# Recurrent mixer: running sums spread over the partitions by bf16 products of three exact pieces, dt from split weights, the selection table written on the chip

## The reference, cut to what matters

```python
proj = h @ w_in
z, xbc, dt, hq, hf, hi, hg = split_cols(proj, [...])        # dt: 8 columns, one for each head
xbc = silu(causal_depthwise_conv_2(xbc, conv_w, conv_b))
...
dt = softplus(dt.astype(F32) + dt_bias.astype(F32))
a_head = -exp(a_log.astype(F32))
a = (dtc * a_head...)                                        # 8 heads x 256 tokens
a_cs = cumsum(a, axis=-1)
seg = exp(where(causal, a_cs[..., :, None] - a_cs[..., None, :], -inf))
y_diag = einsum('bcgls,bcgrls,bcsgrp->bclgrp', cb, seg, xh)
```

## Time and profile before

| | |
|---|---|
| median of 3 runs | 971.42 us (971.24 to 971.78) |
| profiled execution | span 969.5 us; its whole time is not among the numbers, the runs lie 1.9 us above the span |
| PE busy | 951.9 us, 98% |
| DVE, ACT, POOL busy | 697.7, 521.5, 85.5 us |
| recurrent mixer | about 641 to 775 us of the span |

### The profile page before, as it was taken

The page is one execution under the profiler, slowest core; times in us unless marked ns, Lnnn a source line. Parts: engine busy times, 40 slices in busy tenths (PEclk is TensorE's granted clock), DMA queues, the critical chain, the costliest instruction groups (busy, mean ns, idle before and its releaser), DMA issues.

```text
span 969.5 us, 13640 instructions
## 1 busy us (share of the span) xinstructions
PE 951.9 (98%) x5566; PEld 833.2 (86%) x5566; DVE 697.7 (72%) x922; ACT 521.5 (54%) x707; POOL 85.5 (9%) x110
## 2 busy tenths in 40 slices
PE   9999999999999999999999999999999999999997
PEld 8998888888888798789988888888988798888885
DVE  5889866666658977877676666667989777666663
ACT  5888564444446556865444434368555454443432
POOL 2541100000011100000000000000132110000000
PEclk9999999999999999999999999999999999999999
DMA  9922566556645454145655565557322446756531
GB/s 302 318 94 98 191 222 217 174 182 205 198 153 196 129 165 171 47 131 174 217 174 188 186 192 178 168 172 216 114 88 75 143 143 213 224 184 193 181 122 44
DMA packets 106190, 164.40 MB, mean 170 GB/s; under 512 B 2816, under 2 KB 82784, under 8 KB 106000
## 3 DMA queue, kind: packets, MB, share of 16 engines
q1 hardware_dynamic: 104688, 158.25, 50.8%
q0 software_dynamic: 1440, 5.28, 1.5%
HBM read 162.47 MB, written 1.05 MB: 169 GB/s over the span
## 4 chain that ended last, share of the span: by engine, by line
PE 80%; DVE 12%; ACT 4%; issue 2%; POOL 1%; DMA 0%; SPq 0%; DVEq 0%; ACTq 0%
PE ps L379 78%; DVE wl L1770 3%; PE ps L387 2%; ACT xhl L1195 1%; ACT junk L1177 1%; POOL st L2559 1%; DVE st L2192 1%; DVE xf L1791 1%; DVE xhl L1787 1%; DVE rows L2395 1%; DVE h L1844 1%; DVE hs L1802 1%; DMA prm<-in_prm 0%; ACT SC L1515 0%; DVE hs L2406 0%
## 5 line engine op out<-in xcount | busy, mean ns | idle before, releaser
L1770 DVE TENSOR_TENSOR wl<-raw,wh 128x2048 fp32r<-128x2048 f32 (+2 forms) x146 | 329.8, 2262 | 142.0 <-ACT wh L1189 141.8
L1189 ACT ACTIVATE wh<-raw 128x2048 fp32r<-128x2048 f32 (+2 forms) x150 | 281.8, 1884 | 151.7 <-PE ps L379 144.1
L379 PE MATMUL ps<-xhl,wh 128*128 128x512 f32 (+1 forms) x1248 | 254.7, 350 | 0.3 <-ACT wh L1254 0.3
L379 PEld LDWEIGHTS ps<-xhl,wh 128*128 128x128 f32 x1248 | 199.3, 190 | 27.8 <-issue 1.1
L379 PE MATMUL ps<-wh,xhl 128*128 128x512 f32 (+3 forms) x1000 | 195.5, 339 | 1.6 <-issue 0.9
L379 PEld LDWEIGHTS ps<-wh,xhl 128*128 128x128 f32 x1000 | 155.3, 190 | 20.4 <-issue 1.3
L379 PEld LDWEIGHTS ps<-xhl,wl 128*128 128x128 f32 x1008 | 135.7, 191 | 7.5
L379 PE MATMUL ps<-xhl,wl 128*128 128x256 f32 x1008 | 140.6, 282 | 0.0
L379 PE MATMUL ps<-wl,xhl 128*128 128x512 f32 (+3 forms) x500 | 105.4, 336 | 1.0 <-DVE wl L1770 0.9
L379 PE MATMUL ps<-wh,fh 128*128 128x512 f32 x304 | 91.3, 392 | 1.0 <-DVE fl L2034 0.7
L379 PE MATMUL ps<-wh,fl 128*128 128x512 f32 x304 | 90.4, 390 | 0.0
(11 more groups left out here) (274 smaller groups left out, 840.0 us busy)
## 6 DMA issues: line engine op xcount, KB each, us to landing
raw<-in_ffn_gate SPq DMA_DIRECT2D x22, 1024.0 KB, 5.5
raw<-in_ffn_up SPq DMA_DIRECT2D x22, 1024.0 KB, 5.5
raw<-in_ffn_down SPq DMA_DIRECT2D x22, 1024.0 KB, 4.9
raw<-in_w_up SPq DMA_DIRECT2D x16, 1024.0 KB, 5.6
raw<-in_w_down SPq DMA_DIRECT2D x16, 1024.0 KB, 5.0
raw<-in_s_w_in SPq DMA_DIRECT2D x14, 1024.0 KB, 5.4
raw<-in_w_in SPq DMA_DIRECT2D x9, 1024.0 KB, 9.5
raw<-in_a_w_in SPq DMA_DIRECT2D x6, 1024.0 KB, 5.3
```

The costliest lines, as they stand in the source:

```text
L379: return e.matmul(o, a, b, start=start, stop=stop, skip_group_check=True)
L1189: e.activation(high_of(i), raw_of(i), ACT.Copy).then_inc(*up("act_high", i))
L1770: e.tensor_tensor(low_of(i), raw_of(i), high_of(i).bitcast(F32), ALU.subtract).then_inc(*up("dve_lo", i))
```

## The change

Three parts. (1) dt: ACT rounds `wdt` (64 columns) to `wdt_h`, the DVE takes the rest to `wdt_l`, and the PE makes three passes of eight fp32r products with 128 columns of weights each (8 wanted, the rest zeros or other rows that nobody reads). (2) seg: POOL cuts the 8 x 256 running sums into three bf16 pieces in four dependent steps; the first piece lies in rows 0 to 7 of `T3`, the DVE copies the others to rows 32 to 39 and 64 to 71; `sel` has ones in these three rows for a head, so one bf16 product adds the pieces in float32. (3) The float32 table leaves `cst` (1600 columns that POOL's queue loads become 576), `prm` grows from 201 to 209 columns, and POOL writes `sel` (128 x 1024 bf16) and zeros to `T3` and the tails of `wdt_h` and `wdt_l` at the start of the first MLP.

```diff
 # PE, recurrent
-                e.wait_ge(*at("dma_wdt"))
-                e.wait_ge(*at("dve_h", 5, 1, 1))
-                for k in range(8):
-                    d = mm(ps[0][0:8, 0:256], wdt[:, k, :], xf[:, k, :], k == 0, k == 7)
+                for n, (w, x) in enumerate(((wdt_h, xh), (wdt_h, xl), (wdt_l, xh))):
+                    if n != 1:
+                        e.wait_ge(*(at("dve_dt_low") if n else at("act_dt_high")))
+                    for k in range(8):
+
+                        d = mm(ps[0][:, 0:256], w[:, 8 * k:8 * k + 128], x[:, k, :], n == 0 and k == 0, n == 2 and k == 7)
...
                 def seg(i):
-                    o, sel = ps[SEG_BANK[i]], cst[:, C_SEL + 128 * i:C_SEL + 128 * i + 128]
+
+                    o = ps[SEG_BANK[i]]
+                    if i == 0:
+                        e.wait_ge(*at("pool_sel"))
+                        e.wait_ge(*at("pool_seg_high"))
+                        e.wait_ge(*at("dve_seg_rows", 1))
...
-                    mm(o[:, 0:256], sel, T2, True, False)
+                    mm(o[:, 0:256], sel[:, i, :], T3[:, :], True, False)
                     mm(o[:, 0:128], idb[:, :], mtb[:, :], False, True)
-                    mm(o[:, 256:384], sel, T2[:, 128:256], True, False)
+                    mm(o[:, 256:384], sel[:, i, :], T3[:, 128:256], True, False)
 # ACT, after norm_high(5, 1)
+                e.wait_ge(*at("dma_wdt"))
+                e.wait_ge(*at("pool_zero_pieces"))
+                e.activation(wdt_h[:, 0:64], wdt, ACT.Copy).then_inc(*up("act_dt_high"))
 # DVE, before the wait for pe_dt
+                e.wait_ge(*at("act_dt_high"))
+                e.tensor_tensor(wdt_l[:, 0:64], wdt, wdt_h[:, 0:64].bitcast(F32), ALU.subtract).then_inc(*up("dve_dt_low"))
 # DVE, after conv(0)
+                e.wait_ge(*at("pool_seg_rest"))
+                for i, x in enumerate((middle, rest)):
+                    e.tensor_copy(T3[32 + 32 * i:40 + 32 * i, :], x[R, :]).then_inc(*up("dve_seg_rows", i))
 # POOL, after the load of pT (first MLP)
+            e.tensor_copy(sel[:, :, :], P("sel", 0, 8).unsqueeze(2).to_broadcast([128, 8, 128])).then_inc(*up("pool_sel"))
+            for x in (wdt_h, wdt_l):
+                e.memset(x[:, 64:184].bitcast(F32), 0.0)
+            e.memset(T3[:, :], 0.0).then_inc(*up("pool_zero_pieces"))
 # POOL, after the load of hm (recurrent mixer)
+            R = slice(0, 8)
+            e.wait_ge(*at("dve_dt_sum"))
+            e.tensor_copy(T3[R, :], T2[R, :]).then_inc(*up("pool_seg_high"))
+            e.wait_ge(*at("pool_seg_high"))
+            e.tensor_tensor(rest[R, :], T2[R, :], T3[R, :], ALU.subtract).then_inc(*up("pool_seg_left"))
+            e.wait_ge(*at("pool_seg_left"))
+            e.tensor_copy(middle[R, :], rest[R, :]).then_inc(*up("pool_seg_middle"))
+            e.wait_ge(*at("pool_seg_middle"))
+            e.tensor_tensor(rest[R, :], rest[R, :], middle[R, :], ALU.subtract).then_inc(*up("pool_seg_rest"))
```

More of the change, by code:

```diff
@@ L24 @@
 TAPS = 31
-C_ID, C_MA, C_MT, C_ONE, C_SEL, C_ROPE = 0, 128, 256, 384, 512, 1536
+C_ID, C_MA, C_MT, C_ONE, C_ROPE = 0, 128, 256, 384, 512
 C_N = C_ROPE + 2 * 96
@@ L33 @@
           ("qn", 3), ("kvn", 2), ("subln", 1), ("s_norm", 4), ("g_norm", 1), ("lb0", 4), ("lb1", 4),
-          ("bf", 1), ("dtb", 1), ("alog", 1), ("fsel", 4), ("eps", 1), ("mhalf", 4)]
+          ("bf", 1), ("dtb", 1), ("alog", 1), ("fsel", 4), ("eps", 1), ("mhalf", 4), ("sel", 8)]
 P_AT = {}
@@ L48 @@
                       "act_exp act_map_turned act_latent_out act_back"),
-    "act_recurrent": ("act_bound act_hq act_forget act_keys act_log_forget act_rate act_z act_hi act_decay act_between "
+    "act_recurrent": ("act_bound act_dt_high act_hq act_forget act_keys act_log_forget act_rate act_z act_hi act_decay act_between "
                       "act_xbc act_hg act_xb act_xs act_cb act_seg act_gated_square act_silu"),
@@ L56 @@
                       "dve_map dve_map_diff dve_diff_out dve_latent_x dve_latent_low dve_k_rope dve_mix2_low"),
-    "dve_recurrent": ("dve_bound dve_forget_gate dve_keys dve_floor dve_ones dve_decay_sum dve_dt_rate dve_dt_ones "
+    "dve_recurrent": ("dve_bound dve_dt_low dve_seg_rows dve_forget_gate dve_keys dve_floor dve_ones dve_decay_sum dve_dt_rate dve_dt_ones "
                       "dve_dt_sum dve_dt_cumulated dve_score dve_weighed dve_conv_tap dve_conv dve_dt_turned dve_decayed "
@@ L148, in program @@
         mtb = sb("mtb", [128, 128], BF16)
+        sel = sb("sel", [128, 8, 128], BF16)
+        T3 = sb("T3", [128, 256], BF16)
+        middle = sb("middle", [128, 256], BF16)
+        rest = sb("rest", [128, 256])
+        wdt_h, wdt_l = (sb(n, [128, 184], F32R) for n in ("wdt_h", "wdt_l"))
         st = sb("st", [128, 96])
@@ L248, in program @@
         At = fl_f[:, 1280:1360].rearrange("p (a b) -> p a b", a=2)
-        wdt = fl_f[:, 1360:1424].rearrange("p (a b) -> p a b", a=8)
+        wdt = fl_f[:, 1360:1424]
         ones = QK[:, 0, 0:256]
@@ L2702, in constants @@
     c[:, C_ONE:C_ONE + 128] = f(1.0 / 256)
-    for n in range(8):
-        c[n, C_SEL + 128 * n:C_SEL + 128 * n + 128] = 1
     pos = np.arange(256, dtype=f)
@@ L2757 @@
         prm[i, P_AT["fsel"] + i] = prm[32 + i, P_AT["fsel"] + i] = 1
+    for n in range(8):
+        prm[n:96:32, P_AT["sel"] + n] = 1
     prm[:, P_AT["eps"]] = EPS
```

## The result

The changed kernel takes 973.21 us (median of 9 runs; without one disturbed run at 5372 us, which is left out from here on, 973.19), the kernel before 971.55 (9 runs, 971.24 to 971.78): a ratio of 1.0024, 95% interval 1.0015 to 1.0032. The eight runs that are left have two levels, which the kernel before hasn't: five at 973.02 to 973.21 and three at 974.70 to 974.95. The profiled execution is one of the lower level (973.16, span 971.4); so I took the two apart: **some 1.5 us that every run pays** (the middle of the lower five is 973.06; 1.6 by the traces), and **another 1.7 to 1.8 us that some pay**.

What follows compares the result with a forecast made beforehand. The PE sets the end up to 709.8 us, then the DVE; ahead of cb the PE has 1.0 us of room. Mixer +0.66 and first MLP +0.05 make +0.7 on 971.4: 972.1 us, range 970.3 to 973.7.

Steps and rivals of the forecast that it cites:

- sel and the fills in the first MLP: POOL's cast starts after the DVE's L1770 ends, fills only write: cost 0 to 0.2 us, taken as 0.05.
- if the DVE's row around 121 us grows by over 0.3: One of three signs that the prediction is wrong, at the start of the first MLP.
- the PE's wait ahead of cb: In the recurrent mixer, PE waits for ACT some 2 us where there was no wait before.
- POOL's steps: Two subtractions and two casts from 667.4 us in the recurrent mixer, 2.45 us together.
- price d: DVE time lost beside POOL's steps from 667.4 us: 1.5 us, 0.61 of their time; bounds 0.5 to 2.9.
- the standstill of the rival: DVE stands still for the whole of each POOL step it meets: 2.45 us lost, time 973.1; chance 0.15.
- The copies: Two 8 x 256 copies on the DVE after conv(0): 0.45 us, all falling on the last SiLU.
- The DVE took back 0.28: DVE's wait for ACT at 673.39 us follows the PE, now early, so 0.28 us of the loss returns.
- The scans of G: DVE scans in the recurrent mixer, at 675.8 us before, were to come 1.2 us later.
- The last SiLU: ACT's step after the convolution, needed by cb: 1.67 us later, at hand at 702.51.
- cb: late by 0.66: PE's cb waits for the last SiLU, 702.51 against 701.85 us; the first weigh moves by the same 0.66 us.
- seg(2) to seg(7): Some 3 us less PE time in the ladder, where the DVE has no room: taken as 0.

Runs made afterwards that it cites:

- experiment 1: Kernel before plus only POOL's unused 128 x 1024 cast behind the load of pT: 973.07 us; with a fill of that size instead: 972.22 us.
- late table: Changed kernel with POOL's cast of sel and fills behind one more wait, well into the first MLP: seven runs at 971.35 to 971.84 us, four at 972.87 to 972.99.

## Why the prediction was wrong, and where it was right

**The failed step** is "*sel and the fills in the first MLP* ... it starts when that has ended ... Cost 0 to 0.2, I take 0.05". It measured 1.6 us (experiment 1), which is the whole loss that every run pays. I took the order from the rows of before: L1770 starts at 118.84, the cast can't start before the load of pT is issued (its record says 119.38), so the DVE would be first. That order was turned over by a step that I hadn't looked at, the pair on hs at 118.04. Its second half is held until about 119.2 (experiment 1, by cast and fill alike), so L1770 comes to its turn only at 119.63, behind the cast, and stands still for the cast's rest. Half of the loss is the pair, half is L1770, and the forecast had the wrong engine wait. That POOL's step holds the pair before its own recorded start was in no row of before; that no wait guards the cast against the DVE's critical steps was to be seen in the code, and I gave a step that isn't guarded a bound (0 to 0.2) that holds only for one that is. The prediction's own mark, "if the DVE's row around 121 us grows by over 0.3", is the one that was hit.

The rule of the Trainium skill ("SBUF — State Buffer", "Who interferes with whom"), that the second of two such instructions blocks fully until the first has ended, is borne out here in both directions (DVE 3.12 us with the cast first, cast 2.65 us with the DVE first). The section also says that a DVE step with two SBUF inputs contends with a GpSimd step that reads SBUF and not with one that only writes it; cast and fill in experiment 1 agree (3.12 against 2.27). For a `tensor_scalar` in a two-port mode it names no such exception, and the pair took 1.66 with either. The forecast used such an order for the cast too, but with the wrong one first, and gave the fills nothing because they only write.

**A second thing was missing**: the PE's wait ahead of cb was forecast ("2 us or so"; measured 1.99), but taken as free. In part of the runs the granted clock falls behind it, 1.5 us on hq(1) in the late table's trace, and the forecast has no term for it.

**The mixer came out as argued, sizes apart:**
- dt: 0.6 us forecast, 3.55 - 3.00 = 0.55 measured. The pair of seg: 0.7 to 1.1 forecast, 1.70 - 0.56 = 1.14 measured.
- POOL's steps: 2.45 us forecast, 0.50 + 0.72 + 0.39 + 0.67 = 2.28 measured. Their price d for the DVE: 1.5 forecast, 0.36 + 0.67 = 1.03 measured, 0.45 of POOL's time and not 0.61. It isn't the standstill of the rival (2.45): the first cast (0.50) fell beside the DVE's copy and its fill, and beside the other three steps (1.78) the DVE lost 1.03.
- The copies: 0.45 forecast, 0.68 by their rows. The scan's gap (0.36) wasn't forecast. The DVE took back 0.28 by the forecast, and 0.54 by the rows: the subtraction behind the gates starts 4.09 us after the one ahead of it (4.46 before), the scans 2.20 after that one (2.37 before).
- The scans of G: +1.2 forecast, 678.03 - 675.76 - 1.55 = +0.72 measured. The last SiLU: +1.67 forecast, 703.24 - 700.27 - 1.55 = +1.42 measured. cb: late by 0.66 forecast, 0.40 measured. That the two last came so near is in part luck: the port and what the DVE takes back were wrong by 0.7 us to one side, the copies and the scan's gap by 0.6 to the other.
- seg(2) to seg(7): worth 0 forecast. The ladder is 0.2 us shorter for some 3 us less work on the PE, which idles there instead.

So the mixer's +0.3 (in the forecast +0.66) is near nothing, and the late table's lower level (971.52 against 971.47) says the same: 4.8 us of PE time taken out and none gained, since in the ladder the DVE is the limit, and ahead of cb the PE had 1.0 us of room, which dt alone nearly takes (0.76) and the pieces' cost on the DVE takes away again.

**Luck in the total.** The forecast's 972.1 is 1.1 us under the measured 973.2, and not 1.6, because the mixer cost less than forecast. The rival in which the DVE stands still for all of each POOL step gives 973.1, and the range reaches to 973.7; both come near the measured time by a cost of POOL's steps in the mixer of 2.4 us and more, which measured 1.03.

**What was fastest**: dt alone, 970.54 us, 0.85 under the kernel before on the same chip; the copies on ACT with the late table come next (970.65, 0.74 under). Both are within 0.1% of before, and their intervals end at 1.0000 and 1.0001, so this is at the edge of what such runs tell.

## What to carry to other kernels

A step that is "only set-up" on an idle engine is not free by being short: look up which steps of its neighbour on the same port lie around it, the one ahead of the obvious one too, and give it a wait behind the critical one, as one line did here. Shifting such work is no cure where the neighbour has no gap: 1.0 us beside the gates became 1.2 us beside the scans. And time taken from an engine that then waits is not only lost; a wait of 2 us at a place where TensorE sets the end can cost 1.5 us of clock in some of the runs, so look at all runs and not at the median.

## What the runs showed of the hardware that I had not expected

- A POOL fill of 128 x 1024 bf16 (1.22 us) that only writes held the second half of a DVE tensor-scalar pair (0.48 to 1.25 us for that one), and left a tensor-tensor subtraction alone (2.27). The hold on the pair began before the recorded start of POOL's step (119.38), while POOL's DMA issue was on record; the same issue without a step behind it holds nothing (0.88). I have no trace that tells why.
- Four DVE scans beside POOL's steps took 3.65 us for 2.44: these scans, with two SBUF inputs, are held as the subtraction is.
- A POOL cast of 8 x 256 to bf16 takes 0.39 to 0.50 us where no subtraction stands beside it, and 2.32 us when the DVE's came first. The cast of 128 x 1024 takes 1.04 us where the DVE is idle (late table, at 201.30), 1.22 beside the pair and 2.65 behind the subtraction, of which 0.89 lie after the subtraction's end: not all of a POOL record is time in which the DVE is held.
- The granted clock fell in some runs of a kernel and not in others, with the same instructions, behind the same wait.
